# Tail of a hybrid decoder layer: a third gain product moves to GpSimd, the first gate tile's residual add is finished by ScalarE and GpSimd, and the last token tile is added in one pass of 1024 columns

## The chip, the cores and the metric

One core of one Trainium2 chip. The metric is the device time of one execution in microseconds (us), as the median over runs; lower is better.

## The reference

The layer runs an input projection into MoBA attention and gMLP gating, an output projection, a squared-ReLU MLP, and last a gated per-layer embedding (PLE). The change touches only the last of these, for 512 tokens and 1024 columns in float32:

```
gate = jax.nn.sigmoid(jnp.einsum('bsd,de->bse', h, w_ple_gate[i]) + b_ple_gate[i])
ple = jnp.einsum('bsp,pd->bsd', p[i], w_ple[i]) * gate
h = h + rms_norm(ple, ple_post_g[i])          # y * rsqrt(mean(y^2) + eps) * g
```

## The kernel before

The program is written for each engine as one fixed order of instructions, with waits on semaphores between engines. TensorE (PE) does every product in three passes (high by high, low by high, high by low part of a split float32). Nearly the whole of the kernel is a stream of such products.

The last stage works on 512 tokens as four token tiles t of 128 tokens, and on 1024 columns as two halves of W = 512. The gate product is done in seven block products of 2x2 blocks (recombined by sums and differences), each for two token tiles j; the last of them, (6, 1), is done in two parts of 256 columns. Its results come out as nine gate tiles i, numbered in the order in which they are finished:

```
GATE_TILES = ((0, 0, W), (1, 0, W), (2, W, W), (2, 0, W), (3, W, W), (0, W, W), (3, 0, W),
              (1, W, W // 2), (1, W + W // 2, W // 2))      # t, first column, width
TOKENS_DONE = (2, 0, 3, 1)                                  # order in which token tiles complete
```

So token tile 2 is gate tiles 2 and 3, token tile 0 is 0 and 5, token tile 3 is 4 and 6, and token tile 1, the last, is 1, 7 and 8. `GATE_TILES` and the names below are at L289 to L305. Each gate tile goes through these steps:

- `sigmoid(i)`, ScalarE (ACT), L2242: waits for the product in PSUM, or for `gate_c22(j)` on VectorE (tiles 2 and 4). Writes to SBUF (`acc`) for tiles 0 and 1, in place in PSUM for the others.
- `gate_ple(i)`, VectorE (DVE), L1463: times the embedding product, which was spilled to DRAM and loaded back into `ple_late` (SBUF, `ple_of(t)`).
- `square_ple(i)`, ScalarE, L1620: sum of squares (an ACTIVATE and an accumulator read). Each square waits for the one before it, since both write the same scratch tile.
- `gain_ple(i)`, VectorE, L1474: times the norm weight `ple_gain`; for tiles 0 and 1 it is `gain_by_pool(i)` on GpSimd (POOL), L2531, which writes to `ple_of(t)`.
- `partial_sum(i)` and `ple_rstd(t)`, GpSimd, L2512, L2518 and L2520: the sum of squares of a token tile to 1/sqrt of the mean. Two small instructions in `ple_rstd`, the second a power.
- `add_ple(i)`, VectorE, L1486: h = gained * rstd + h, once the token tile's `ple_rstd` is there.
- a store of the tile (L2689), issued by SyncE (SP) in the order 2, 3, 0, 5, 4, 6, 1, 7, 8, each when `out_ready` has counted that add.

What sets the order of the work is the order of these calls on each engine. VectorE also has `gate_c22(1)` (L1440), which releases gate product (5, 1) and `sigmoid(4)`, and `gate_fold(1)` (L1452, L1454), which releases product (6, 1). The calls at the end on VectorE, from `gate_ple(2)` on, are:

```
gate_ple(2) gate_fold(1) gain_ple(2) gate_c22(1) gate_ple(3) gate_ple(4) gain_ple(3) gain_ple(4)
gate_ple(5) add_ple(2) add_ple(3) gain_ple(5) gate_ple(6) add_ple(0) gate_ple(7) add_ple(5)
gain_ple(6) gate_ple(8) gain_ple(7) add_ple(4) gain_ple(8) add_ple(6) add_ple(1) add_ple(7) add_ple(8)
```

Of the kernel before, what the change touches and what calls it, by code (L numbers as in the profile page):

```python
# [35 lines left out]
ALU = mybir.AluOpType  # L36
ACT = mybir.ActivationFunctionType
AXIS_X = mybir.AxisListType.X

P = 128  # L40
# [5 lines left out]
W = 512  # L46
HALVES = D // W
# [24 lines left out]
LAST = STEPS - 1  # L72
# [16 lines left out]
GATE_COPIES = ((COPY_C11, 0), (COPY_C11, 1), (COPY_E, 0), (COPY_CHAIN, 0), (COPY_CHAIN, 1), (COPY_E, 1))  # L89
# [22 lines left out]
def gate_copy_at(which, j):  # L112

    return 3 * LAST + GATE_COPIES.index((which, j)) + 1


def gate_c22_at(j):
# [152 lines left out]
def tail_results():  # L270
# [18 lines left out]
GATE_TILES = ((0, 0, W), (1, 0, W), (2, W, W), (2, 0, W), (3, W, W), (0, W, W), (3, 0, W),  # L289
              (1, W, W // 2), (1, W + W // 2, W // 2))  # L290
TOKENS_DONE = (2, 0, 3, 1)
# [1 line left out]


LAST_GATED = len(GATE_TILES) - 1
GAINED_BY_POOL = (0, 1)


def width_of(i):
# [3 lines left out]
def gate_tiles_of(t):  # L303

    return [i for i, tile in enumerate(GATE_TILES) if tile[0] == t]  # L305
# [10 lines left out]
def hymba_layer(nc, x, xT, pT, weights, columns, rope, ws, rows, out):  # L316
# [6 lines left out]
    with ExitStack() as ctx:  # L323
# [31 lines left out]
        h = place("h", [P, TT, D])  # L355
# [65 lines left out]
        acc = place("acc", [P, TT, D], at=at_area)  # L421
# [40 lines left out]
        def ple_of(t):  # L462
            return ple_late[t // 2][:, t % 2, :]
# [16 lines left out]
        ss_pl, rstd_pl = stat[:, 146:], stat[:, 64:68]  # L480
# [11 lines left out]
        def sem(name):  # L492
            return ctx.enter_context(nc.semaphore(name))
# [9 lines left out]
        stored = sem("stored")  # L503
# [45 lines left out]
        c_summed, c_copied = sem("c_summed"), sem("c_copied")  # L549
# [4 lines left out]
        first_load = 16  # L554
        h2_raw, gate_seeded, gate_folded = sem("h2_raw"), sem("gate_seeded"), sem("gate_folded")
        h_spilled = sem("h_spilled")
        gained_by_pool = sem("gained_by_pool")
        h_loaded = [sem(f"h_loaded{t}") for t in range(TT)]
        t_hi_done, t_lo_done, a_hi_done, a_lo_done = (sem("t_hi_done"), sem("t_lo_done"),
                                                      sem("a_hi_done"), sem("a_lo_done"))  # L560
# [162 lines left out]
        def gate_result(i):  # L723

            t, c0, width = GATE_TILES[i]
            if i == LAST_GATED:
                return psum[:, GATE_LAST_PART, 0:width]
            if t < 2:
                bank = GATE_E if c0 else GATE_P1
            else:  # L730
                bank = GATE_C22 if c0 else GATE_CHAIN
            return psum[:, bank + t % 2, 0:width]

        def gated_of(i):

            t, c0, width = GATE_TILES[i]
            return acc[:, t, 0:W] if i < 2 else gate_result(i)

        def gained_of(i):

            t, c0, width = GATE_TILES[i]
            return ple_of(t)[:, c0:c0 + width] if i in GAINED_BY_POOL else gate_result(i)

        def down_result(t):

# [9 lines left out]
        def _(dve):  # L755
# [564 lines left out]
            for step in range(LAST):  # L1320
                n = PRODUCTS * step
# [135 lines left out]
            def gate_ple(i):  # L1457
                t, c0, width = GATE_TILES[i]
                cut = slice(c0, c0 + width)
                dve.wait_ge(sig_done, i + 1)  # L1460
                if i in (0, 2):
                    dve.wait_ge(ple_loaded[t // 2], 16)
                nc.vector.tensor_tensor(gated_of(i), gated_of(i), ple_of(t)[:, cut], ALU.mult).then_inc(pl_gated, 1)  # L1463

            GAINED = (2, 3, 4, 5, 6, 7, 8)

            def gain_ple(i):

                if i == GAINED[0]:
                    dve.wait_ge(post_loaded, 48)  # L1470
                t, c0, width = GATE_TILES[i]
                cut = slice(c0, c0 + width)
                dve.wait_ge(pl_squared, i + 1)
                nc.vector.tensor_tensor(gained_of(i), gated_of(i), ple_gain[:, cut], ALU.mult  # L1474
                                        ).then_inc(pl_gained, 1)

            def add_ple(i):

                t, c0, width = GATE_TILES[i]
                cut = slice(c0, c0 + width)  # L1480
                dve.wait_ge(pl_rstd, TOKENS_DONE.index(t) + 1)
                if i in GAINED_BY_POOL:
                    dve.wait_ge(gained_by_pool, GAINED_BY_POOL.index(i) + 1)
                else:
                    dve.wait_ge(pl_gained, GAINED.index(i) + 1)
                nc.vector.scalar_tensor_tensor(out=h[:, t, cut], in0=gained_of(i),  # L1486
                                               scalar=rstd_pl[:, t:t + 1], in1=h[:, t, cut],
                                               op0=ALU.mult, op1=ALU.add).then_inc(out_ready, 1)

            def tail_down(d):  # L1490

# [52 lines left out]
            h2_sum_split_lo(OF_S4, 1)  # L1544
            gate_ple(2)
            gate_fold(1)
            gain_ple(2)
            gate_c22(1)
            gate_ple(3)
            gate_ple(4)  # L1550
            gain_ple(3)
            gain_ple(4)
            gate_ple(5)
            add_ple(2)
            add_ple(3)
            gain_ple(5)
            gate_ple(6)
            add_ple(0)
            gate_ple(7)
            add_ple(5)  # L1560
            gain_ple(6)
            gate_ple(8)
            gain_ple(7)
            add_ple(4)
            gain_ple(8)
            add_ple(6)
            add_ple(1)
            add_ple(7)
            add_ple(8)

# [2 lines left out]
        def _(act):  # L1575
# [514 lines left out]
            for step in range(LAST):  # L2090
                n = PRODUCTS * step
# [143 lines left out]
            def sigmoid(i):  # L2235
                t, c0, width = GATE_TILES[i]
                j = t % 2
                if t >= 2 and c0:
                    act.wait_ge(c_summed, gate_c22_at(j))
                else:  # L2240
                    act.wait_ge(up_filled, gate_at(6 if c0 else 1 if t < 2 else 5, j) + (i == LAST_GATED))
                nc.scalar.activation(gated_of(i), gate_result(i), ACT.Sigmoid).then_inc(sig_done, 1)  # L2242

            def square_ple(i):
                t, c0, width = GATE_TILES[i]
                act.wait_ge(pl_gated, i + 1)
                square(gated_of(i), ss_pl[:, i:i + 1], pl_squared)
# [54 lines left out]
            gate_copy(COPY_E, 1)  # L2302
            square_ple(0)
            square_ple(1)
            square_ple(2)
            sigmoid(3)
            sigmoid(4)
            square_ple(3)
            square_ple(4)
            sigmoid(5)  # L2310
            square_ple(5)
            sigmoid(6)
            sigmoid(7)
            square_ple(6)
            sigmoid(8)
            square_ple(7)
            square_ple(8)


# [3 lines left out]
        def _(pool):  # L2323
# [182 lines left out]
            def partial_sum(i):  # L2506

                t = GATE_TILES[i][0]
                partial = ple_partial[:, t:t + 1]
                before = partial if i != gate_tiles_of(t)[0] else D * EPS  # L2510
                pool.wait_ge(pl_squared, i + 1)
                after(nc.gpsimd.tensor_scalar(partial, ss_pl[:, i:i + 1], before, None, ALU.add))  # L2512

            def ple_rstd(t):

                last_tile = gate_tiles_of(t)[-1]
                pool.wait_ge(pl_squared, last_tile + 1)
                after(nc.gpsimd.tensor_scalar(ple_mean, ss_pl[:, last_tile:last_tile + 1], ple_partial[:, t:t + 1],  # L2518
                                              1.0 / D, ALU.add, ALU.mult))
                nc.gpsimd.tensor_tensor(rstd_pl[:, t:t + 1], ple_mean, minus_half[:, 0:1], ALU.pow  # L2520
                                        ).then_inc(pl_rstd, 1)
                pool.wait_ge(pl_rstd, TOKENS_DONE.index(t) + 1)

            def gain_by_pool(i):
                t, c0, width = GATE_TILES[i]
                cut = slice(c0, c0 + width)
                if i == 0:
                    pool.wait_ge(post_loaded, 48)
                    pool.wait_ge(sum_lo_done, gate_sum_split_at(OF_S4, 1))
                pool.wait_ge(pl_gated, i + 1)  # L2530
                nc.gpsimd.tensor_tensor(gained_of(i), gated_of(i), ple_gain[:, cut], ALU.mult  # L2531
                                        ).then_inc(gained_by_pool, 1)

            partial_sum(0)
            partial_sum(1)
            gain_by_pool(0)
            gain_by_pool(1)
            partial_sum(2)
            ple_rstd(2)
            partial_sum(4)  # L2540
            ple_rstd(0)
            ple_rstd(3)
            partial_sum(7)
            ple_rstd(1)
# [5 lines left out]
        def _(sp):  # L2550
            for item in FIRST_ORDER:
                if isinstance(item, str):
                    i = int(item[1:])
                    t, ks = X_PIECES[i]
# [127 lines left out]
            gate_x(GATE_22, 0)  # L2682
            gate_x(GATE_22, 1)
            sp.dma_start(ple_late[1][:], ple_spill[:, 2:4, :]).then_inc(ple_loaded[1], 16)
            order = (2, 3, 0, 5, 4, 6, 1, 7, 8)
            for n, i in enumerate(order):
                t, c0, width = GATE_TILES[i]
                sp.wait_ge(out_ready, n + 1)
                sp.dma_start(out[t * P:(t + 1) * P, c0:c0 + width], h[:, t, c0:c0 + width]  # L2689
                             ).then_inc(stored, 16)  # L2690
            sp.wait_ge(stored, 16 * len(order))

# [590 lines left out]
```

## Time and profile before

| | |
|---|---|
| runs | 578.3, 579.03, 579.38 us; median 579.03 |
| profiled execution | 578.58 us, of which the span from the first to the last instruction is 576.7 us |
| PE busy | 568.4 us, 99% of the span |
| DVE busy | 500.8 us, 87% |
| ACT busy | 374.9 us, 65% |
| POOL busy | 96.2 us, 17% |
| TensorE clock | granted 0.996 of full speed over the span |

Times in the profile are us from the start of the span, durations of single instructions us or ns. In a timeline row the first number is the start, the second the duration (of the whole merged group where it says x2 and more), and what stands in brackets is the idle time of the engine before it and what ended that. VectorE and ScalarE start an instruction a little before the one in front of it has ended, so the step from start to start is shorter than a duration.

### The profile page before, as it was taken

To read this page: it belongs to the slowest core of one execution; us is meant where nothing else is said; L and a number is where in the kernel's file an instruction comes from. 1 tells how busy PE (TensorE), PEld (TensorE's weight loads), DVE (VectorE), ACT (ScalarE), POOL (GpSimd) and SP (SyncE) were. 2 spreads that over 40 slices of the span, in tenths; PEclk is the share of its full clock that TensorE was granted. 3 is DMA by queue.
4 is the path that set the end of the run, shared out by engine and by line. 5 is a ranking of instruction groups with operands and counts; after the bars stand their busy time and mean duration, and the time that the engine had idled before them with its cause. 6 is when DMAs were issued, how large, how long until landed. Compare 5 with 4: busy or idle time off the path is not lost.

```text
span 576.7 us, 8934 instructions
## 1 busy us (share of the span) xinstructions
PE 568.4 (99%) x3364; PEld 496.3 (86%) x3364; DVE 500.8 (87%) x645; ACT 374.9 (65%) x595; POOL 96.2 (17%) x159
## 2 busy tenths in 40 slices
PE   9999999999999999999999999999999999999995
PEld 7888888888888888899999989999998999988884
DVE  5899986688865998999999989999999899798898
ACT  6896674876555747667565565665665656686784
POOL 0321437000102501001000010011010100014122
PEclk9999999999999999999999999999999999999998
DMA  8982008223103497367476384592774853897823
GB/s 268 346 324 90 0 2 321 82 73 108 41 1 110 147 349 233 74 195 207 74 249 154 73 266 100 147 255 44 236 167 77 268 124 78 324 265 144 227 112 148
DMA packets 28603, 93.73 MB, mean 163 GB/s; under 512 B 3216, under 2 KB 4624, under 8 KB 28304
## 3 DMA queue, kind: packets, MB, share of 16 engines
q1 hardware_dynamic: 20736, 67.64, 33.0%
q0 software_dynamic: 5328, 19.14, 18.8%
q10 hardware_dynamic: 2496, 6.37, 3.1%
q8 instruction: 27, 0.44, 0.3%
q14 instruction: 16, 0.13, 0.1%
HBM read 86.85 MB, written 6.29 MB: 161 GB/s over the span
## 4 chain that ended last, share of the span: by engine, by line
PE 93%; DVE 3%; ACT 1%; issue 1%; DMA 1%; DVEq 0%; SPq 0%; ACTq 0%
PE psum L2703 29%; PE psum L2707 29%; PE psum L2708 29%; PE psum L2758 2%; PE psum L2941 2%; PE psum L2921 2%; DVE h L1486 1%; DMA first_raw_a<-weights_dram 1%; PE psum L2772 1%; DVE w_lo L1376 1%; DVE psum L1474 1%; DVE psum L1463 0%; ACT junk_late L1620 0%; PE psum L2795 0%; DVE actT_lo L1432 0%
## 5 line engine op out<-in xcount | busy, mean ns | idle before, releaser
L2703 PE MATMUL psum<-t_hi,a_hi 128*128 128x512 f32 x216 | 84.7, 392 | 0.0
L2707 PE MATMUL psum<-t_lo,a_hi 128*128 128x512 f32 x216 | 84.6, 392 | 0.0
L2708 PE MATMUL psum<-t_hi,a_lo 128*128 128x512 f32 x216 | 84.0, 389 | 0.0
L2703 PE MATMUL psum<-w_hi,actT_hi 128*128 128x512 f32 (+1 forms) x178 | 69.7, 392 | 0.0
L2708 PE MATMUL psum<-w_hi,actT_lo 128*128 128x512 f32 (+1 forms) x178 | 68.5, 385 | 0.0
L2707 PE MATMUL psum<-w_lo,actT_hi 128*128 128x512 f32 (+1 forms) x178 | 68.4, 384 | 0.0
L2708 PE MATMUL psum<-sum_hi,up_lo 128*128 128x256 f32 x224 | 63.4, 283 | 0.0
L2707 PE MATMUL psum<-sum_lo,up_hi 128*128 128x256 f32 x224 | 63.4, 283 | 0.0
L2703 PE MATMUL psum<-sum_hi,up_hi 128*128 128x256 f32 x224 | 63.2, 282 | 0.0
L2708 PE MATMUL psum<-actT_hi,up_lo 128*128 128x256 f32 (+1 forms) x200 | 60.0, 300 | 0.0
L2707 PE MATMUL psum<-actT_lo,up_hi 128*128 128x256 f32 (+1 forms) x200 | 60.0, 300 | 0.0
L2703 PE MATMUL psum<-actT_hi,up_hi 128*128 128x256 f32 (+1 forms) x200 | 59.9, 299 | 0.0
L2454 POOL DMA_DIRECT2D raw_x<-weights_dram x21 | 18.6, 883 | 238.6 <-DVE t_lo L1235 238.6
L1294 DVE TENSOR_TENSOR acc<-acc,psum 128x512 f32<-128x512 f32 x76 | 49.1, 681 | 1.8 <-PE psum L2708 1.8
L2708 PEld LDWEIGHTS psum<-t_hi,a_lo 128*128 128x128 f32 x216 | 40.6, 188 | 8.8
L1090 DVE TENSOR_TENSOR up_lo<-raw,up_hi 128x1024 fp32r<-128x1024 f32 x37 | 45.2, 1220 | 2.6 <-ACT up_hi L1881 2.0
L2703 PEld LDWEIGHTS psum<-t_hi,a_hi 128*128 128x128 f32 x216 | 40.8, 189 | 7.1
L2707 PEld LDWEIGHTS psum<-t_lo,a_hi 128*128 128x128 f32 x216 | 40.8, 189 | 6.6
L2707 PEld LDWEIGHTS psum<-sum_lo,up_hi 128*128 128x128 f32 x224 | 42.9, 191 | 1.1
L2703 PEld LDWEIGHTS psum<-sum_hi,up_hi 128*128 128x128 f32 x224 | 42.9, 191 | 1.1
L2708 PEld LDWEIGHTS psum<-sum_hi,up_lo 128*128 128x128 f32 x224 | 42.9, 191 | 0.0
L2707 PEld LDWEIGHTS psum<-actT_lo,up_hi 128*128 128x128 f32 x200 | 38.2, 191 | 2.0
(290 smaller groups left out, 1438.0 us busy)
## 6 DMA issues: line engine op xcount, KB each, us to landing
raw<-weights_dram SPq DMA_DIRECT2D x40, 512.0 KB, 4.8
raw_o<-weights_dram SPq DMA_DIRECT2D x23, 512.0 KB, 4.3
raw_x<-weights_dram POOLq DMA_DIRECT2D x21, 512.0 KB, 5.6
raw_second<-weights_dram SPq DMA_DIRECT2D x16, 512.0 KB, 4.1
raw_x<-weights_dram SPq DMA_DIRECT2D x9, 512.0 KB, 6.1
qk_raw<-weights_dram SPq DMA_DIRECT2D x8, 512.0 KB, 7.8
raw_o<-weights_dram POOLq DMA_DIRECT2D x7, 512.0 KB, 6.9
raw_second<-weights_dram POOLq DMA_DIRECT2D x6, 512.0 KB, 6.6
```

Source lines behind the costliest of these rows:

```text
L1090: nc.vector.tensor_tensor(up_lo[q % UP_SLOTS][:], block_source(step, j), up_hi[q % UP_SLOTS][:].bitcast(F32), ALU.subtract).then_inc(block ...
L1294: nc.vector.tensor_tensor(part, part, bank, how).then_inc(product_added, 1)
L1376: nc.vector.tensor_tensor(gate_half(low, part), gate_source(block, part), gate_half(high, part).bitcast(F32), ALU.subtract).then_inc(block ...
L1474: nc.vector.tensor_tensor(gained_of(i), gated_of(i), ple_gain[:, cut], ALU.mult).then_inc(pl_gained, 1)
L1486: nc.vector.scalar_tensor_tensor(out=h[:, t, cut], in0=gained_of(i), scalar=rstd_pl[:, t:t + 1], in1=h[:, t, cut], op0=ALU.mult, op1=ALU.a ...
L2454: nc.gpsimd.dma_start(raw_x[step % 2][:], weights[down_in_stream(step, rows, half)], accum_op=ALU.add).then_inc(x_added, 16)
L2703: begin = nc.tensor.matmul(out, a_hi, b_hi, start=first, stop=False, skip_group_check=read_between)
L2707: nc.tensor.matmul(out, a_hi, b_lo, start=False, stop=False, skip_group_check=read_between)
L2708: return nc.tensor.matmul(out, a_lo, b_hi, start=False, stop=last, skip_group_check=read_between)
L2758: mm = nc.tensor.transpose(psum[:, banks[name], j * P:(j + 1) * P], source[:, j * P:(j + 1) * P], ident[:])
L2921: mm = nc.tensor.transpose(psum[:, bank + s, k * P:(k + 1) * P], probs[:, place_in_group(unit), s, k * P:(k + 1) * P], ident[:])
L2941: mm = nc.tensor.matmul(psum[s * DH:(s + 1) * DH, BANK_O, pair * P:(pair + 1) * P], v[:, k, head * DH:(head + 1) * DH], probsT_of[place_in ...
```

## The change

`gain_ple(2)` goes from VectorE to GpSimd (`GAINED_BY_POOL` becomes (0, 1, 2)); since GpSimd reads SBUF, `gate_ple(2)` now writes to `acc`. The add of tile 0 leaves VectorE: ScalarE multiplies by rstd (`scale_gained(0)`, between `sigmoid(6)` and `sigmoid(7)`) and GpSimd adds h (`add_by_pool(0)`, between `ple_rstd(0)` and `ple_rstd(3)`). The three adds of token tile 1 become one of 1024 columns (`add_last`), for which `gain_ple(7)` and `gain_ple(8)` write to `ple_of(1)`; its store goes out as two of 512 columns, issued one behind the other. The order of the calls changes on VectorE and on ScalarE.

```diff
-GAINED_BY_POOL = (0, 1)
+GAINED_BY_POOL = (0, 1, 2)
+ADDED_BY_POOL = (0,)
+LAST_TOKENS = TOKENS_DONE[-1]
...
+            def add_last():
+                t = LAST_TOKENS
+                dve.wait_ge(pl_rstd, TOKENS_DONE.index(t) + 1)
+                dve.wait_ge(tail_by_pool, GAINED_BY_POOL.index(gate_tiles_of(t)[0]) + 1)
+                dve.wait_ge(pl_gained, len(GAINED))
+                nc.vector.scalar_tensor_tensor(out=h[:, t, :], in0=ple_of(t), scalar=rstd_pl[:, t:t + 1],
+                                               in1=h[:, t, :], op0=ALU.mult, op1=ALU.add).then_inc(out_ready, 1)
...
             gate_fold(1)
-            gain_ple(2)
+            gate_ple(3)
             gate_c22(1)
-            gate_ple(3)
+            gain_ple(3)
             gate_ple(4)
-            gain_ple(3)
-            gain_ple(4)
-            gate_ple(5)
             add_ple(2)
             add_ple(3)
+            gate_ple(5)
+            gain_ple(4)
             gain_ple(5)
             gate_ple(6)
-            add_ple(0)
+            add_ple(5)
             gate_ple(7)
-            add_ple(5)
             gain_ple(6)
+            gain_ple(7)
             gate_ple(8)
-            gain_ple(7)
             add_ple(4)
             gain_ple(8)
             add_ple(6)
-            add_ple(1)
-            add_ple(7)
-            add_ple(8)
+            add_last()
...
+            def scale_gained(i):
+                t = GATE_TILES[i][0]
+                act.wait_ge(pl_rstd, TOKENS_DONE.index(t) + 1)
...
+                nc.scalar.activation(scaled_of(i), gained_of(i), ACT.Copy, scale=rstd_pl[:, t:t + 1]
+                                     ).then_inc(c_copied, 1)
...
             square_ple(0)
             square_ple(1)
+            sigmoid(3)
             square_ple(2)
-            sigmoid(3)
+            square_ple(3)
             sigmoid(4)
-            square_ple(3)
             square_ple(4)
             sigmoid(5)
             square_ple(5)
             sigmoid(6)
+            scale_gained(0)
             sigmoid(7)
             square_ple(6)
+            square_ple(7)
             sigmoid(8)
-            square_ple(7)
             square_ple(8)
...
+            def add_by_pool(i):
+                t, c0, width = GATE_TILES[i]
+                cut = slice(c0, c0 + width)
+                pool.wait_ge(c_copied, GATE_SCALED + ADDED_BY_POOL.index(i))
+                nc.gpsimd.tensor_tensor(h[:, t, cut], scaled_of(i), h[:, t, cut], ALU.add
+                                        ).then_inc(tail_by_pool, 1)
...
             partial_sum(2)
+            gain_by_pool(2)
             ple_rstd(2)
             partial_sum(4)
             ple_rstd(0)
+            add_by_pool(0)
             ple_rstd(3)
...
-            order = (2, 3, 0, 5, 4, 6, 1, 7, 8)
+            order = (2, 3, 5, 0, 4, 6)
...
+            sp.wait_ge(out_ready, len(added_by_dve) + 1)
+            for half in range(HALVES):
+                cut = slice(half * W, (half + 1) * W)
+                sp.dma_start(out[LAST_TOKENS * P:(LAST_TOKENS + 1) * P, cut], h[:, LAST_TOKENS, cut]
+                             ).then_inc(stored, 16)
```

## Rows read from the trace of the kernel before

**Rows 1.** The page: busy time of two engines over the span.

```profile
PE 568.4 (99%) x3364; PEld 496.3 (86%) x3364; DVE 500.8 (87%) x645; ACT 374.9 (65%) x595; POOL 96.2 (17%) x159
```

**Rows 2.** Timeline of TensorE: last matmuls of products (4,1) and (6,1).

```profile
561.04 0.39 PE L2708 MATMUL psum<-w_hi,actT_lo 128*128 128x512 f32 x1
...
569.46 0.28 PE L2708 MATMUL psum<-w_hi,actT_lo 128*128 128x256 f32 x1
```

**Rows 3.** Timeline of VectorE from 560 us to its end.

```profile
560.26 0.42 DVE L1454 TENSOR_TENSOR psum<-psum,acc 128x256 f32<-128x256 f32 x1
...
561.54 0.70 DVE L1440 TENSOR_TENSOR psum<-acc,psum 128x512 f32<-128x512 f32 x1
562.14 1.44 DVE L1463 TENSOR_TENSOR psum<-psum,ple_late_b 128x512 f32<-128x512 f32 x2
563.59 1.48 DVE L1474 TENSOR_TENSOR psum<-psum,ple_gain 128x512 f32<-128x512 f32 x2
564.98 0.69 DVE L1463 TENSOR_TENSOR psum<-psum,ple_late_a 128x512 f32<-128x512 f32 x1
565.57 1.40 DVE L1486 SCALAR_TENSOR_TENSOR h<-psum,stat,h 128x512 f32<-128x512 f32 x2
...
571.70 0.42 DVE L1474 TENSOR_TENSOR psum<-psum,ple_gain 128x256 f32<-128x256 f32 x1
572.03 0.74 DVE L1486 SCALAR_TENSOR_TENSOR h<-psum,stat,h 128x512 f32<-128x512 f32 x1
572.69 0.74 DVE L1486 SCALAR_TENSOR_TENSOR h<-ple_late_a,stat,h 128x512 f32<-128x512 f32 x1
573.35 0.87 DVE L1486 SCALAR_TENSOR_TENSOR h<-psum,stat,h 128x256 f32<-128x256 f32 x2
```

**Rows 4.** Timeline of ScalarE over the same stretch (L2242 sigmoid, L1620 square).

```profile
565.70 0.60 ACT L1620 ACTIVATE junk_late<-psum 128x512 f32<-128x512 f32 x1 [0.88 <-DVE psum L1463]
566.19 0.19 ACT L1620 ACTIVATION_READ_ACCUMULATOR junk_late<-psum 128x1 f32 x1
566.91 0.58 ACT L2242 ACTIVATE psum<-psum 128x512 f32<-128x512 f32 x1 [0.52 <-PE psum L2708]
568.34 0.37 ACT L2242 ACTIVATE psum<-psum 128x256 f32<-128x256 f32 x1 [0.85 <-PE psum L2708]
```

**Rows 5.** Timeline of GpSimd (L2531 gain_by_pool, L2512 partial_sum, L2518 and L2520 ple_rstd).

```profile
559.64 2.55 POOL L2531 TENSOR_TENSOR ple_late_a<-acc,ple_gain 128x512 f32<-128x512 f32 x2 [0.17 <-POOL stat L2512]
562.16 0.21 POOL L2512 TENSOR_SCALAR stat<-stat 128x1 f32<-128x1 f32 x1
563.73 0.27 POOL L2518 TENSOR_SCALAR stat<-stat 128x1 f32<-128x1 f32 x1 [1.35 <-ACT junk_late L1620]
564.08 0.57 POOL L2520 TENSOR_TENSOR stat<-stat 128x1 f32<-128x1 f32 x1
571.83 0.57 POOL L2520 TENSOR_TENSOR stat<-stat 128x1 f32<-128x1 f32 x1
```

**Rows 6.** Groups by line and shape: two forms that the change adds.

```profile
L1395 DVE SCALAR_TENSOR_TENSOR acc<-acc,stat,mlp_gain 128x1024 f32<-128x1024 f32 x1 | 1.3, 1284 | 0.7 <-POOL stat L2354 0.7
L1586 ACT ACTIVATE w_hi<-raw,cols x32: 706/713/730, 18.1 to 141.9; 128x512 fp32r<-128x512 f32 x32
```

**Rows 7.** Timeline of the SP queue: the first store's issue, and the last two.

```profile
566.34 0.34 SPq L2689 DMA_DIRECT2D out_dram<-h  x1
573.86 0.94 SPq L2689 DMA_DIRECT2D out_dram<-h  x2
```

**Rows 8.** DMA issues in the last 4 us: size of each, us to landing.

```profile
out_dram<-h SPq DMA_DIRECT2D x2, 256.0 KB, 2.0
out_dram<-h SPq DMA_DIRECT2D x2, 128.0 KB, 2.1
```

**Rows 9.** Stretches: busy us of PE, PEld, DVE, ACT, POOL; clock; DMA share, GB/s.

```profile
566.30:567.10 0.80, 0.80 (x7) 0.72 (x6) 0.80 (x3) 0.28 (x2) 0.46 (x2) 1.00 0.00 0
567.10:567.80 0.70, 0.70 (x9) 0.70 (x8) 0.70 (x2) 0.39 (x1) 0.38 (x1) 1.00 0.88 345
```

More of the change, by code:

```diff
@@ L114, in gate_copy_at @@
     return 3 * LAST + GATE_COPIES.index((which, j)) + 1
+GATE_SCALED = 3 * LAST + len(GATE_COPIES) + 1
 def gate_c22_at(j):
@@ L295 @@
 LAST_GATED = len(GATE_TILES) - 1
-GAINED_BY_POOL = (0, 1)
+GAINED_BY_POOL = (0, 1, 2)
+ADDED_BY_POOL = (0,)
+LAST_TOKENS = TOKENS_DONE[-1]
+GAINED = (3, 4, 5, 6, 7, 8)
 def width_of(i):
@@ L556, in hymba_layer @@
         h_spilled = sem("h_spilled")
-        gained_by_pool = sem("gained_by_pool")
+        tail_by_pool = sem("tail_by_pool")
         h_loaded = [sem(f"h_loaded{t}") for t in range(TT)]
@@ L736, in gated_of, with sigmoid_of, scaled_of @@
             t, c0, width = GATE_TILES[i]
+            if i == 2:
+                return acc[:, t, c0:c0 + width]
             return acc[:, t, 0:W] if i < 2 else gate_result(i)
+        def sigmoid_of(i):
+            return gated_of(i) if i < 2 else gate_result(i)
         def gained_of(i):
             t, c0, width = GATE_TILES[i]
-            return ple_of(t)[:, c0:c0 + width] if i in GAINED_BY_POOL else gate_result(i)
+            kept = i in GAINED_BY_POOL or t == LAST_TOKENS
+            return ple_of(t)[:, c0:c0 + width] if kept else gate_result(i)
+        def scaled_of(i):
+            t, c0, width = GATE_TILES[i]
+            return ple_of(t)[:, c0:c0 + width]
         def down_result(t):
@@ L1462, in gate_ple @@
                     dve.wait_ge(ple_loaded[t // 2], 16)
-                nc.vector.tensor_tensor(gated_of(i), gated_of(i), ple_of(t)[:, cut], ALU.mult).then_inc(pl_gated, 1)
-            GAINED = (2, 3, 4, 5, 6, 7, 8)
+                nc.vector.tensor_tensor(gated_of(i), sigmoid_of(i), ple_of(t)[:, cut], ALU.mult).then_inc(pl_gated, 1)
             def gain_ple(i):
@@ L1482, in add_ple @@
                 if i in GAINED_BY_POOL:
-                    dve.wait_ge(gained_by_pool, GAINED_BY_POOL.index(i) + 1)
+                    dve.wait_ge(tail_by_pool, GAINED_BY_POOL.index(i) + 1)
                 else:
@@ L2241, in sigmoid @@
                     act.wait_ge(up_filled, gate_at(6 if c0 else 1 if t < 2 else 5, j) + (i == LAST_GATED))
-                nc.scalar.activation(gated_of(i), gate_result(i), ACT.Sigmoid).then_inc(sig_done, 1)
+                nc.scalar.activation(sigmoid_of(i), gate_result(i), ACT.Sigmoid).then_inc(sig_done, 1)
+            def scale_gained(i):
+                t = GATE_TILES[i][0]
+                act.wait_ge(pl_rstd, TOKENS_DONE.index(t) + 1)
+                if i in GAINED_BY_POOL:
+                    act.wait_ge(tail_by_pool, GAINED_BY_POOL.index(i) + 1)
+                else:
+                    act.wait_ge(pl_gained, GAINED.index(i) + 1)
+                nc.scalar.activation(scaled_of(i), gained_of(i), ACT.Copy, scale=rstd_pl[:, t:t + 1]
+                                     ).then_inc(c_copied, 1)
             def square_ple(i):
@@ L2531, in gain_by_pool @@
                 nc.gpsimd.tensor_tensor(gained_of(i), gated_of(i), ple_gain[:, cut], ALU.mult
-                                        ).then_inc(gained_by_pool, 1)
+                                        ).then_inc(tail_by_pool, 1)
+            def add_by_pool(i):
+                t, c0, width = GATE_TILES[i]
+                cut = slice(c0, c0 + width)
+                pool.wait_ge(c_copied, GATE_SCALED + ADDED_BY_POOL.index(i))
+                nc.gpsimd.tensor_tensor(h[:, t, cut], scaled_of(i), h[:, t, cut], ALU.add
+                                        ).then_inc(tail_by_pool, 1)
             partial_sum(0)
@@ L2684, in _ @@
             sp.dma_start(ple_late[1][:], ple_spill[:, 2:4, :]).then_inc(ple_loaded[1], 16)
-            order = (2, 3, 0, 5, 4, 6, 1, 7, 8)
-            for n, i in enumerate(order):
+            order = (2, 3, 5, 0, 4, 6)
+            added_by_dve = [i for i in order if i not in ADDED_BY_POOL]
+            for i in order:
                 t, c0, width = GATE_TILES[i]
-                sp.wait_ge(out_ready, n + 1)
+                if i in ADDED_BY_POOL:
+                    sp.wait_ge(tail_by_pool, len(GAINED_BY_POOL) + ADDED_BY_POOL.index(i) + 1)
+                else:
+                    sp.wait_ge(out_ready, added_by_dve.index(i) + 1)
                 sp.dma_start(out[t * P:(t + 1) * P, c0:c0 + width], h[:, t, c0:c0 + width]
                              ).then_inc(stored, 16)
-            sp.wait_ge(stored, 16 * len(order))
+            sp.wait_ge(out_ready, len(added_by_dve) + 1)
[3 more added lines that the diff above has]
+                             ).then_inc(stored, 16)
+            sp.wait_ge(stored, 16 * (len(order) + HALVES))
         @block.tensor
```

## The prediction

> **What bounds the kernel now.** I read the page first: TensorE is busy for 99% of the span [rows 1]. So only the time behind its last product can change, unless the edit makes TensorE wait. Next the timeline of TensorE: the last matmul starts at 569.46 and ends at 569.74 [rows 2], and the span ends at 576.7. What lies in those 7 us is the drain of the last tiles. The timeline of VectorE [rows 3] shows it working almost without a gap from 560 us to its last add, which ends at 573.35 + 0.87 = 574.22. GpSimd's last `ple_rstd` ends at 571.83 + 0.57 = 572.40 [rows 5], while the first add that needs it starts only at 572.69 [rows 3]: VectorE's backlog, by 0.3 us, and not the norm, sets the end. The SP queue issues the last store at about 574.34 (the last two issues take 0.94 together from 573.86, some 0.45 of it the second) [rows 7]; it lands 2.0 to 2.1 later, at 576.4 [rows 8], and the span ends 0.3 after that.
>
> **Prices from the rows.** VectorE, from start to start: 0.60 for 512 columns of tensor_tensor (561.54 to 562.14), 0.33 for 256 (571.70 to 572.03), 0.66 for an add of 512 (572.69 to 573.35) [rows 3]. ScalarE [rows 4]: sigmoid 0.58, of 256 columns 0.37; a square of 512 is complete 0.68 after its start (565.70 to 566.38), and the next instruction that isn't a square starts some 0.1 before that. GpSimd: a product of 512 columns 1.26 from start to start (559.64 to 562.16 for two), `ple_rstd` 0.92 from its first start to the end of its power (563.73 to 564.65) [rows 5]. A wait between engines costs 0.04, and 0.17 into GpSimd (566.38 is the square's end in [rows 4]; the 0.17 is the bracket of the first row in [rows 5]).
>
> **What is removed.** From VectorE: `gain_ple(2)` 0.60, `add_ple(0)` 0.66, and the three last adds, 0.66 + 0.87 = 1.53, become one of 1024 columns. The trace has that form at L1395, 1.28 [rows 6], so 0.25 less. In all 1.51 us of VectorE's work. If that were all, the last add would end at 572.7.
>
> **Why it can't end there.** The last rstd is not made by VectorE. Its chain is last matmul 569.74, sigmoid(8), gate_ple(8), square_ple(8), `ple_rstd(1)`, and it ended at 572.40 [rows 5], 2.66 after the matmul, with nothing in it that the edit shortens. `add_last` needs it before its first column. So it ends at 572.40 + 0.05 + 1.28 = 573.73 at best, 0.5 before today's 574.22, and not 1.5.
>
> **What the new order does, step by step.** I place each instruction behind its engine's last one and behind its releaser.
>
> VectorE to 564.7: `gate_fold(1)` as before, its second part at 560.26 [rows 3]; `gate_ple(3)` 560.59 (sigmoid(3) now runs before square_ple(2), so it is there); `gate_c22(1)` at 561.54 as before, because product (4, 1) ends at 561.04 + 0.39 = 561.43 [rows 2]; so the place freed by `gain_ple(2)` is partly empty already. `gain_ple(3)` 562.14, `gate_ple(4)` at 562.88, as before (the second of the pair from 562.14 ends at 563.58 and takes 0.70, it waits for sigmoid(4)) [rows 3]. Now comes `add_ple(2)`, which waits for `ple_rstd(2)`. On GpSimd the new product fills the gap in front of it: `partial_sum(2)` 562.16, `gain_by_pool(2)` 562.45 to 563.7, `ple_rstd(2)` 563.71 to 564.64, the time it also had before (564.08 + 0.57) [rows 5]. So GpSimd pays nothing for the gain, but VectorE, which had two gains and `gate_ple(5)` in front of this add, has nothing: it stands idle from 563.48 to 564.70, 1.2 us. Queued behind are add 2, add 3 and, behind these, `gate_ple(5)`, at 564.70 + 2 x 0.66 = 566.02 in place of 564.98 [rows 3].
>
> For `gate_ple(5)` wait square_ple(5) and all that stands behind it on ScalarE. Square 566.74 to 567.43 (before 565.70 to 566.38) [rows 4]. `ple_rstd(0)` 567.60 to 568.52. sigmoid(6) 567.33 to 567.91. `scale_gained(0)` waits for that rstd: 568.56. Its form, Copy with a scale per partition, stands at L1586 with 0.71 [rows 6]: to 569.27. Queued behind it is sigmoid(7), at 569.18 against 568.34 before [rows 4], then square_ple(6) 569.46 to 570.15, square_ple(7) 570.23 to 570.69, sigmoid(8) 570.58 to 570.95. The last product is there at 569.74, so sigmoid(8) is 0.8 late.
>
> VectorE meanwhile: `gain_ple(4)` 566.62, `gain_ple(5)` 567.47 (waits for its square, 0.25 idle), `gate_ple(6)` 568.07, add 5 568.67, `gate_ple(7)` 569.59 (waits for sigmoid(7)), `gain_ple(6)` 570.19 (square_ple(6)), `gain_ple(7)` 570.79, `gate_ple(8)` 571.12 to 571.55. Square_ple(8) is complete at 572.04.
>
> GpSimd: `add_by_pool(0)` after scale_gained, 569.44 to 570.70. The trace has no GpSimd add, but a product of the same shape with the same two SBUF inputs [rows 5]; I take 1.26, with 0.9 and 1.6 as the ends; VectorE gets to add 4 at 571.45, so that the shorter gains only 0.2 and the longer costs 0.34. Behind it is `ple_rstd(3)`, 570.70 to 571.62; add 4 waits for it, at 571.66. Then `gain_ple(8)` 572.32, add 6 572.65, `add_last` at 573.31. `ple_rstd(1)` (572.21 to 573.13) is in time for it. It ends at 573.31 + 1.28 = **574.59, 0.37 later than before**: 1.5 us of work removed; 1.2 us of idle ahead of add 2 and 1.0 in four small waits (ahead of `gain_ple(5)`, `gate_ple(7)`, `gain_ple(6)` and add 4) put in; the rest, some 0.3, are small waits that the old order had. TensorE isn't touched: `gate_c22(1)` and `gate_fold(1)`, which release its last products, stay where they were.
>
> **The stores.** The first half is issued at 574.62, the second 0.34 to 0.45 behind it (the length of an issue) [rows 7]. A store of 256 KB alone lands after 2.0 [rows 8]: nothing moves for 0.8 us after the issue at 566.34, then the engines fill [rows 9]. The 345 GB/s of the next stretch at a share of 0.88 [rows 9] make some 390 at full share, by which 256 KB need 0.67 us, so the second half waits for the first and lands some 2.0 + 0.65 = 2.65 after the first issue; without that queueing at 2.34. So 576.96 to 577.3, I take 577.25. Before, the last piece was 128 KB, landing at 576.4, 2.2 behind its add. Cost of the stores: 0.04 + 2.65 against 2.2: 0.5.
>
> The Trainium skill (DMA: Bandwidth & Descriptors, Anatomy of one DMA) fits a DMA as a fixed 2.0 us plus bytes over 436 GB/s; a 256 KB store would land after 2.6 by it, and both halves after some 3.2. The trace has 2.0 and 2.1 for 256 and 128 KB, where the rule would want 0.3 between them, so I go by the rows.
>
> **Sum.** Against the profiled execution: +0.37 for the last add, +0.5 for the stores, some +0.85 in all: a span of 577.5, and 579.4 for its execution, which lay 0.45 under the median. Against the median 579.03 it is 579.03 + 0.8 = **579.8 us**. What a measurement of this kernel can tell from no change is 0.2%, or 1.16 us, so this is "no change", on its slow side.
>
> **Rivals.** (1) *VectorE packs without the waits.* From add 2 at 564.70 the remaining work is 5 adds (3.3), 5 products of 512 (3.0), 4 of 256 (1.3) and the 1.28: 8.9, so 573.6; with the floor 573.73 and stores of 2.65 it gives 576.4, the same as before: -0.3 to +0.3, 579.0. For it: each small wait is 0.2 to 0.3 and could vanish. Against: scale_gained(0) can't run before the chain through `gate_ple(5)`, which is late for certain. Chance 0.16.
> (2) *Slower by more than 0.2%: GpSimd becomes the bound.* It now carries 2.5 us more at two places on which an idle VectorE waits: each 0.1 us that `gain_by_pool(2)` takes above 1.26 delays `ple_rstd(2)` and add 2 by as much, and all behind them. It decides from 0.31 us on: 0.85 + 0.31 = 1.16. If both took 1.6 it would be 0.34 at each, 579.03 + 0.85 + 0.68 = 580.6. Against: the two products of before took 1.26 each beside a busy VectorE [rows 5]. Chance 0.15. The Trainium skill (GPSIMD Engine Reference, Specifications) says that GpSimd shares its SBUF interfaces with VectorE and contends with VectorE instructions that have two SBUF inputs; VectorE has none such beside either of the new ones in the order above.
> (3) *The two halves add their whole latency.* If the second lands 3.3 after the first issue, the end is 0.65 later, +1.5 us, 580.5. The landing of 2.0 for a lone 256 KB speaks against it [rows 8]; the skill's rule above would come near it. Chance 0.06.
> (4) *Faster by over 0.2%.* It takes the last add and the last landing to be 1.16 earlier, below the floor of 573.73 + 2.38, 576.1, which is only 0.3 under today's 576.4. Only a spread between runs could show it. Chance 0.04.
> The forecast itself, +0.3 to +1.15, has 0.59.
>
> **The numbers.** Faster 0.04. Same: 0.59 + 0.16 and 0.01 of the rest, 0.76. Slower: 0.20. The range takes in rival 1 below and most of 2 and 3 above, and the 578.3 to 579.38 of the runs: 578.5 to 580.7.
>
> **What would show it.** Right: VectorE idle by about 1.2 us ahead of the first L1486 row, released by GpSimd; sigmoid(7) some 0.8 later than 568.34, behind an ACTIVATE of 0.7; the 1024-column add of about 1.28 starting at or after 573.0; a second store landing about 2.65 after the first issue; TensorE's last matmul unmoved. Wrong: TensorE's end moves (a late `gate_fold` or `gate_c22`), the idle ahead of add 2 is under 0.5, or the 1024-column add starts by 572.6.

## The result and the profile after

| | us |
|---|---|
| before, 20 runs | median 578.59 (578.18 to 580.02) |
| changed, 20 runs | median 579.57 (578.99 to 580.5) |
| ratio | 1.0016, 95% interval 1.001 to 1.0022 |
| profiled execution of the changed kernel | 580.29, span 578.5 |

The changed kernel is slower by 0.16%, some 0.9 us. That is clear of zero, and inside the 0.2% up to which the prediction counted "no change".

The timeline of VectorE after (L1483 is `gate_ple`, L1492 `gain_ple`, L1504 `add_ple`, L1514 `add_last`, L1460 `gate_c22`); it answers to [rows 3]:

```profile
560.27 0.68 DVE L1483 TENSOR_TENSOR acc<-psum,ple_late_b 128x512 f32<-128x512 f32 x1
...
562.13 0.68 DVE L1460 TENSOR_TENSOR psum<-acc,psum 128x512 f32<-128x512 f32 x1
563.04 0.70 DVE L1492 TENSOR_TENSOR psum<-psum,ple_gain 128x512 f32<-128x512 f32 x1 [0.23 <-ACT junk_late L1643]
563.65 0.69 DVE L1483 TENSOR_TENSOR psum<-psum,ple_late_b 128x512 f32<-128x512 f32 x1
565.63 0.75 DVE L1504 SCALAR_TENSOR_TENSOR h<-ple_late_b,stat,h 128x512 f32<-128x512 f32 x1 [1.30 <-POOL stat L2554]
566.30 0.74 DVE L1504 SCALAR_TENSOR_TENSOR h<-psum,stat,h 128x512 f32<-128x512 f32 x1
566.97 0.69 DVE L1483 TENSOR_TENSOR psum<-psum,ple_late_a 128x512 f32<-128x512 f32 x1
...
570.53 0.43 DVE L1483 TENSOR_TENSOR psum<-psum,ple_late_a 128x256 f32<-128x256 f32 x1 [0.17 <-ACT psum L2265]
...
572.54 0.75 DVE L1504 SCALAR_TENSOR_TENSOR h<-psum,stat,h 128x512 f32<-128x512 f32 x1
...
574.20 1.28 DVE L1514 SCALAR_TENSOR_TENSOR h<-ple_late_a,stat,h 128x1024 f32<-128x1024 f32 x1
```

The row to see first is the add at 565.63. In its bracket stand 1.30 us of idle time, ended by GpSimd: add 2 waits for `ple_rstd(2)`. The `gate_ple(5)` at 566.97 stands behind it in VectorE's queue. The timelines of ScalarE and GpSimd show where that goes (L2265 sigmoid, L2274 `scale_gained`, L2565 `gain_by_pool`, L2572 `add_by_pool`, L2554 the power of `ple_rstd`); they answer to [rows 4, 5]:

```profile
567.69 0.60 ACT L1643 ACTIVATE junk_late<-psum 128x512 f32<-128x512 f32 x1 [2.14 <-DVE psum L1483]
...
568.27 0.59 ACT L2265 ACTIVATE psum<-psum 128x512 f32<-128x512 f32 x1
569.50 0.72 ACT L2274 ACTIVATE ple_late_a<-ple_late_a,stat 128x512 f32<-128x512 f32 x1 [0.64 <-POOL stat L2554]
570.13 0.36 ACT L2265 ACTIVATE psum<-psum 128x256 f32<-128x256 f32 x1
```

```profile
563.40 1.30 POOL L2565 TENSOR_TENSOR ple_late_b<-acc,ple_gain 128x512 f32<-128x512 f32 x1
564.67 0.27 POOL L2552 TENSOR_SCALAR stat<-stat 128x1 f32<-128x1 f32 x1
565.03 0.57 POOL L2554 TENSOR_TENSOR stat<-stat 128x1 f32<-128x1 f32 x1
...
570.37 1.26 POOL L2572 TENSOR_TENSOR h<-ple_late_a,h 128x512 f32<-128x512 f32 x1 [0.90 <-ACT ple_late_a L2274]
```

ScalarE sits idle for 2.14 us until `gate_ple(5)` comes, then for 0.64 until the norm of token tile 0 is there, and only behind `scale_gained(0)` comes sigmoid(7). GpSimd has no idle time between its product and `ple_rstd(2)`: the product stands right in front of it.

At the end the timeline of the SP queue (L2741 issues the two halves of the last store), and that line's durations in ns, starts and times to landing, answering to [rows 7, 8]:

```profile
575.51 0.81 SPq L2741 DMA_DIRECT2D out_dram<-h  x2
```

```profile
L2741 SPq DMA_DIRECT2D out_dram<-h x2: 333/383/433, 575.5 to 575.9; - x2
...
DMA to landing us min/median/max: 2.0/2.1/2.2
```

The add ends at 574.20 + 1.28 = 575.48, the halves are issued at 575.5 and 575.9, and the second takes 2.2 to land.

To set this profile against the one of before, two marks are wanted. The timeline of TensorE has its last matmul, answering to [rows 2]:

```profile
569.93 0.28 PE L2760 MATMUL psum<-w_hi,actT_lo 128*128 128x256 f32 x1
```

It ends at 570.21, 0.47 later than before, and `gate_ple(2)` starts at 560.27, 0.94 later (559.33 in the trace of before). Neither is the change's doing. Long before its place, an accumulating load of gate weights (issued by GpSimd at 527.1, 512 KB) landed later in this execution, and ScalarE and VectorE, and in the end TensorE's weight load, waited for it. The DMA issues (KB, us to landing), the timeline of ScalarE and VectorE, and the waits (us in total, times, longest):

```profile
raw_second<-weights_dram POOLq DMA_DIRECT2D x1, 512.0 KB, 12.9
```

```profile
540.09 1.06 ACT L2169 ACTIVATE w_hi<-raw_second 128x1024 fp32r<-128x1024 f32 x1 [1.50 <-DMA raw_second<-weights_dram]
...
541.18 1.22 DVE L1396 TENSOR_TENSOR w_lo<-raw_second,w_hi 128x1024 fp32r<-128x1024 f32 x1 [1.87 <-ACT w_hi L2169]
```

```profile
PEld psum L2755 <- DVE actT_lo L1452: 0.8, 1, 0.8
```

In the profile of before the same load landed after 11.7 us and ScalarE waited for 0.28. The timelines of ScalarE and VectorE there (L1463 is `gate_ple`):

```profile
539.14 1.06 ACT L2146 ACTIVATE w_hi<-raw_second 128x1024 fp32r<-128x1024 f32 x1 [0.28 <-DMA raw_second<-weights_dram]
...
540.23 1.22 DVE L1376 TENSOR_TENSOR w_lo<-raw_second,w_hi 128x1024 fp32r<-128x1024 f32 x1 [0.65 <-ACT w_hi L2146]
...
559.33 0.69 DVE L1463 TENSOR_TENSOR psum<-psum,ple_late_b 128x512 f32<-128x512 f32 x1
```

VectorE's row at 541.18 stands at 540.23 here, so the whole delay, 0.95, is present before the first instruction that the change touches. Four kernels below (two adds, both mends, rstd first, product doubled), which have the same order of work up to here, but whose load landed after 10.9 to 12.1, start their last matmul at 569.32 to 569.44 against 569.46 before, and the profile shows no wait of TensorE for another engine from 545 us on. The reordered kernel and that with tile 0 on VectorE, where it landed after 12.6 and 12.4, start it late, like the changed one, at 570.20 and 570.05. The profiled execution, 580.29, lies 0.7 above its own median; the late load is the likely reason, but the other executions left no profile that could show it. In the text below, times in the tail are given against the end of the last matmul, or against `gate_ple(2)`, and each says which.

### The profile page after: what moved, and what is told of

Same layout as the page of the kernel before. It is cut to its first block, busy times and chain, and to the rows that moved or that the text cites. A ratio compares the mean times of both kernels' runs of the same rounds, so it can differ in the third digit from the quotient of the medians.

```text
span 578.5 us, 8930 instructions
## 1 busy us (share of the span) xinstructions
PE 568.6 (98%) x3364; PEld 496.4 (86%) x3364; DVE 499.5 (86%) x641; ACT 375.4 (65%) x596; POOL 99.3 (17%) x161
## 4 chain that ended last, share of the span: by engine, by line
PE 86%; DMA 3%; DVE 3%; ACT 2%; POOL 2%; issue 1%; DVEq 0%; POOLq 0%; ACTq 0%
PE psum L2755 27%; PE psum L2759 26%; PE psum L2760 26%; DMA raw_second<-weights_dram 2%; PE psum L2993 2%; PE psum L2810 2%; PE psum L2973 2%; DMA raw<-weights_dram 1%; DVE w_lo L1396 1%; PE psum L2864 1%; ACT w_hi L2169 1%; PE psum L2824 1%; POOL ple_late_a L2565 0%; POOL stat L2388 0%; PE psum L2847 0%
```

## The experiments

Eight kernels were timed, each against runs of the kernel before on the same chip, in 11 or 12 runs each, the doubled product in 5. Theory 1 is the prediction's own: an idle VectorE ahead of add 2, with `gate_ple(5)` and the chain to sigmoid(7) behind it, costs upstream, and the stores cost at the end. "Behind" is the end of the last add less the end of the last matmul, and "tail" the end of the span less that of the last matmul.

| kernel | ratio to before, interval | behind | tail |
|---|---|---|---|
| before | | 4.48 | 6.96 |
| changed | 1.0016, 1.001 to 1.0022 | 5.27 | 8.29 |
| reordered | 0.9997, 0.9988 to 1.0006 | 4.05 | 7.12 |
| tile 0 on VectorE | 1.002, 1.001 to 1.0029 | 5.31 | 8.37 |
| last add alone | 1.0006, 0.9997 to 1.0015 | 4.23 | 7.24 |
| two adds | 1.0008, 0.9999 to 1.0017 | 5.30 | 7.70 |
| reordered, two adds | 0.9984, 0.9975 to 0.9993 | 3.99 | 6.40 |
| rstd first, two adds | 0.9988, 0.9979 to 0.9997 | 4.09 | 6.48 |
| product doubled | 1.0033, 1.0021 to 1.0046 | 6.09 | 9.15 |
| product alone | 1.0000, 0.9991 to 1.0009 | 4.48 | 7.05 |

**Reordered.** The changed kernel with two VectorE instructions moved:

```diff
             gate_ple(4)
+            gain_ple(4)
+            gate_ple(5)
             add_ple(2)
             add_ple(3)
-            gate_ple(5)
-            gain_ple(4)
             gain_ple(5)
```

> The changed kernel with gain_ple(4) and gate_ple(5) ahead of add_ple(2) on VectorE, as in the order of before. Theory 1 (the loss upstream is VectorE idling ahead of add_ple(2) for ple_rstd(2), with gate_ple(5) and the whole chain to sigmoid(7) queued behind it): most of that idle is filled, scale_gained(0) and sigmoid(7) come some 1 us earlier against the last matmul, the 1024-column add starts on the release of the last ple_rstd, 4.0 us or less after the end of the last matmul less its own 1.28, i.e. it ends 3.9 to 4.2 us behind the last matmul instead of 5.3; the time is 0.9 us under the changed kernel, about that of before (ratio to before 0.999 to 1.001). Rival (the detour of tile 0 over ScalarE and GpSimd costs the time by itself): idle goes, but the last add still ends over 4.8 behind the last matmul, ratio 1.001 to 1.002.

VectorE's timeline:

```profile
565.38 0.70 DVE L1492 TENSOR_TENSOR psum<-psum,ple_gain 128x512 f32<-128x512 f32 x1 [0.75 <-ACT junk_late L1643]
565.99 0.69 DVE L1483 TENSOR_TENSOR psum<-psum,ple_late_a 128x512 f32<-128x512 f32 x1
566.59 0.74 DVE L1504 SCALAR_TENSOR_TENSOR h<-ple_late_b,stat,h 128x512 f32<-128x512 f32 x1
...
573.25 1.28 DVE L1514 SCALAR_TENSOR_TENSOR h<-ple_late_a,stat,h 128x1024 f32<-128x1024 f32 x1
```

Add 2 no longer waits; 0.75 are left ahead of `gain_ple(4)`, which needs its square. The last add ends 4.05 behind the last matmul, in the middle of the forecast, with the detour of tile 0 untouched. It starts right behind add 6 and not on the release of the last norm, as expected, which had ended 0.14 earlier. The median is 578.37 against 578.49 of before: the order of two instructions was all of the loss upstream. The rival's 1.001 to 1.002 lie above the interval, and it falls.

**Tile 0 on VectorE.** The changed kernel without the detour:

```diff
-ADDED_BY_POOL = (0,)
+ADDED_BY_POOL = ()
...
             gate_ple(6)
+            add_ple(0)
+            gate_ple(7)
             add_ple(5)
-            gate_ple(7)
...
             sigmoid(6)
-            scale_gained(0)
             sigmoid(7)
...
             ple_rstd(0)
-            add_by_pool(0)
             ple_rstd(3)
...
-            order = (2, 3, 5, 0, 4, 6)
+            order = (2, 3, 0, 5, 4, 6)
```

> The changed kernel with tile 0's add back on VectorE (scale_gained and add_by_pool gone, add_ple(0) behind gate_ple(6)). Theory 1: the detour only occupies engines that wait anyway, since gate_ple(5) is late in both; sigmoid(7) comes earlier but VectorE has 0.66 more to do, so the last add ends within 0.2 us of where it ends in the changed kernel, 5.1 to 5.4 behind the last matmul, ratio to before 1.001 to 1.002. Rival (the detour is what costs): last add at least 0.5 earlier, ratio 1.000 to 1.001.

VectorE's timeline, `gate_ple(7)` and the last add:

```profile
570.39 0.43 DVE L1483 TENSOR_TENSOR psum<-psum,ple_late_a 128x256 f32<-128x256 f32 x1
...
574.36 1.28 DVE L1514 SCALAR_TENSOR_TENSOR h<-ple_late_a,stat,h 128x1024 f32<-128x1024 f32 x1
```

The last add ends 5.31 behind, against 5.27, and the ratio is 1.002. So the detour neither costs nor saves here. The 0.66 it takes from VectorE comes back as waits: in the changed kernel VectorE stands for 0.26 ahead of `gate_ple(7)`, 0.27 ahead of `gain_ple(6)` and 0.14 ahead of add 4, and here ahead of none of the three.

**Last add alone.** The kernel before with only `add_last` and its two stores (and `gain_ple(7)`, `gain_ple(8)` writing to `ple_of(1)`):

```diff
             add_ple(6)
-            add_ple(1)
-            add_ple(7)
-            add_ple(8)
+            add_last()
...
-            order = (2, 3, 0, 5, 4, 6, 1, 7, 8)
+            order = (2, 3, 0, 5, 4, 6)
...
+            for half in range(HALVES):
+                cut = slice(half * W, (half + 1) * W)
+                sp.dma_start(out[P:2 * P, cut], h[:, 1, cut]).then_inc(stored, 16)
...
```

> The kernel before with only the last part of the change: one add of 1024 columns for token tile 1 and two stores of 512 columns behind it. Theory 1: the add starts where the first of the three did (behind add_ple(6), about 2.95 us after the end of the last matmul) and ends 0.25 us earlier than the three did, but both halves are stored behind it, the second lands some 2.65 behind the first issue against 2.2 behind the last add before; net +0.2 to +0.3 us, ratio 1.0000 to 1.0008. Rival (the single pass and wide stores pay): -0.25 us, ratio 0.9992 to 1.000.

VectorE's timeline:

```profile
573.01 1.28 DVE L1496 SCALAR_TENSOR_TENSOR h<-ple_late_a,stat,h 128x1024 f32<-128x1024 f32 x1
```

The single pass ends 4.23 behind in place of 4.48, 0.25 earlier as priced; the tail is 0.28 longer all the same. The ratio's interval holds 1, so the sign rests on the two profiles, where the size is the one forecast.

**Two adds.** The changed kernel with the last tile in two passes:

```diff
-                nc.vector.scalar_tensor_tensor(out=h[:, t, :], in0=ple_of(t), scalar=rstd_pl[:, t:t + 1],
-                                               in1=h[:, t, :], op0=ALU.mult, op1=ALU.add).then_inc(out_ready, 1)
+                for half in range(HALVES):
+                    cut = slice(half * W, (half + 1) * W)
+                    nc.vector.scalar_tensor_tensor(out=h[:, t, cut], in0=ple_of(t)[:, cut], scalar=rstd_pl[:, t:t + 1],
+                                                   in1=h[:, t, cut], op0=ALU.mult, op1=ALU.add).then_inc(out_ready, 1)
...
-            sp.wait_ge(out_ready, len(added_by_dve) + 1)
             for half in range(HALVES):
+                sp.wait_ge(out_ready, len(added_by_dve) + half + 1)
```

> The changed kernel with the last tile added in two passes of 512 columns, each stored behind its own. Theory 1 (the stores cost because both wait for the whole add): the first half is issued 0.6 us earlier, the second add ends 0.12 later than the single pass, the second store is not queued behind the first and lands 2.0 after its issue: the end comes 0.5 us earlier against the last matmul than in the changed kernel; ratio to before about 1.0005 to 1.001. Rival (the stores' landing is fixed and the number of issues counts): no change or +0.1 us, ratio 1.0016.

The last add ends where it did (5.30; counted from `gate_ple(2)`, 15.33 against 15.21, it is the 0.12 later that was expected), but the tail is 7.70 and not 8.29: 0.59 less. The ratio, 1.0008, is in the range of theory 1, but its interval reaches 1.0017 and so holds the rival's 1.0016: what decides is the two profiles. The timeline of the SP queue, and the same line's durations, starts and landings:

```profile
574.26 0.99 SPq L2743 DMA_DIRECT2D out_dram<-h  x2
```

```profile
L2743 SPq DMA_DIRECT2D out_dram<-h x2: 332/332/332, 574.3 to 574.9; - x2
...
DMA to landing us min/median/max: 2.0/2.0/2.0
```

Issued 0.66 apart, each half lands after 2.0; issued 0.4 apart, the second took 2.2. The second half is issued 5.3 behind the last matmul in place of 5.7: of what is won, 0.4 is the earlier issue and 0.2 the shorter landing.

**Both mends together.** The edits of "reordered" and of "two adds" in one kernel.

> Both mends together: the changed kernel with gain_ple(4) and gate_ple(5) ahead of add_ple(2), and the last tile added in two passes of 512 columns with a store behind each. Theory 1 (the two costs are separate and add up): last add some 4.2 us behind the last matmul, its store lands 2.0 after its issue, the span ends 6.4 to 6.6 behind the last matmul against 6.96 before; ratio to before 0.999 to 0.9995. Rival (the tail is bound by something neither edit touches): no better than the reordered kernel alone, ratio 0.9995 to 1.0003.

Rows of the timelines of ScalarE, GpSimd (the last norm), VectorE and SP:

```profile
568.30 0.37 ACT L2267 ACTIVATE psum<-psum 128x256 f32<-128x256 f32 x1
...
571.68 0.57 POOL L2556 TENSOR_TENSOR stat<-stat 128x1 f32<-128x1 f32 x1
...
572.28 1.41 DVE L1516 SCALAR_TENSOR_TENSOR h<-ple_late_a,stat,h 128x512 f32<-128x512 f32 x2
...
573.06 0.99 SPq L2743 DMA_DIRECT2D out_dram<-h  x2
```

Sigmoid(7) is back at 568.30 (568.34 before), the first of the last adds starts at 572.28. The tail is 6.40 where 6.4 to 6.6 was forecast, 0.56 shorter than before. The runs, 577.71 to 578.06, lie all below the lowest of the kernel before beside them, 578.22. The ratio, 0.9984, is 0.0006 better than the best expected; the profiles account for 0.56 us of the 0.8 between the medians, and where the rest comes from stays open.

**Rstd first.** `gain_by_pool(2)` behind `ple_rstd(2)`, and VectorE's order to suit, with the two adds:

```diff
-            gain_by_pool(2)
             ple_rstd(2)
+            gain_by_pool(2)
...
             gate_ple(4)
-            add_ple(2)
             add_ple(3)
-            gate_ple(5)
             gain_ple(4)
+            gate_ple(5)
+            add_ple(2)
             gain_ple(5)
...
-            order = (2, 3, 5, 0, 4, 6)
+            order = (3, 2, 5, 0, 4, 6)
```

> The changed kernel with ple_rstd(2) ahead of gain_by_pool(2) on GpSimd, add 3 in the gap on VectorE, then gain_ple(4), gate_ple(5), add 2; and the last tile in two passes. Theory 1: ple_rstd(2) ends 1.3 us earlier (it waited on GpSimd only for the product in front of it), add 3 fills the gap, gate_ple(5) is back at its old place; from there the floor of the last ple_rstd sets the end, so it equals the run with both mends within 0.2 us, ratio 0.999 to 0.9995. Rival (ple_rstd(2) is bound by its square and not by the product): ple_rstd(2) no earlier, add 3 waits 1 us, ratio 1.000 to 1.001.

The timelines of GpSimd and, for the last adds, of VectorE:

```profile
562.85 0.27 POOL L2554 TENSOR_SCALAR stat<-stat 128x1 f32<-128x1 f32 x1
563.20 0.57 POOL L2556 TENSOR_TENSOR stat<-stat 128x1 f32<-128x1 f32 x1
563.85 1.30 POOL L2567 TENSOR_TENSOR ple_late_b<-acc,ple_gain 128x512 f32<-128x512 f32 x1
...
571.70 0.57 POOL L2556 TENSOR_TENSOR stat<-stat 128x1 f32<-128x1 f32 x1
```

```profile
571.74 0.74 DVE L1504 SCALAR_TENSOR_TENSOR h<-psum,stat,h 128x512 f32<-128x512 f32 x1
572.40 1.41 DVE L1516 SCALAR_TENSOR_TENSOR h<-ple_late_a,stat,h 128x512 f32<-128x512 f32 x2
```

On GpSimd the norm now ends at 563.77, 4.07 behind `gate_ple(2)` (559.70) where it was 5.33 (565.60 less 560.27): 1.26 earlier, just the product. It was the product, not the square, that held it. The time is about that of the kernel with both mends (0.9988 against 0.9984, again a little better than the range expected, but with an interval that reaches into it). The last norm ends 2.55 behind the last matmul in both. There the first of the last adds starts 0.03 behind it, on the floor; here it starts 0.13 behind it, at 572.40, right behind add 6. So with both mends in, an earlier `ple_rstd(2)` finds nothing left to win.

**Product doubled.** The changed kernel with `gain_by_pool(2)` issued twice, to the same place, the second behind the end of the first:

```diff
+                if i == 2:
+                    after(nc.gpsimd.tensor_tensor(gained_of(i), gated_of(i), ple_gain[:, cut], ALU.mult))
```

> The changed kernel with gain_by_pool(2) issued twice. Theory 1 (add_ple(2) waits on GpSimd's queue, without slack, and all behind it with it): VectorE's idle ahead of add_ple(2) grows from 1.3 to 2.6 us, the last add ends 1.2 to 1.4 later against the last matmul, ratio to before 1.0035 to 1.0042. Rival (the idle is slack that later work takes up): last add under 0.5 later, ratio 1.0016 to 1.0025.

VectorE's timeline:

```profile
561.45 0.70 DVE L1460 TENSOR_TENSOR psum<-acc,psum 128x512 f32<-128x512 f32 x1 [0.33 <-PE psum L2762]
...
565.90 0.75 DVE L1504 SCALAR_TENSOR_TENSOR h<-ple_late_b,stat,h 128x512 f32<-128x512 f32 x1 [2.41 <-POOL stat L2554]
...
574.47 1.27 DVE L1514 SCALAR_TENSOR_TENSOR h<-ple_late_a,stat,h 128x1024 f32<-128x1024 f32 x1
```

The idle time ahead of add 2 is 2.41, where 2.6 was expected. Counted from `gate_ple(2)` (559.17 here) the last add ends after 16.57, against 15.21: 1.36 later, in full. Counted from the last matmul it is only 0.82 later, less than the 1.2 expected, because VectorE as a whole ran earlier in this execution: the accumulating load had landed after 10.9. The time is some 1.0 above the changed kernel's by the ratios (1.0033 less 1.0016), between the theories and nearer to the first. Counted from `gate_ple(2)`, a delay on GpSimd passes through to the last add without slack; the time agrees, but its interval (1.0021 to 1.0046) holds part of the rival's range too.

**Product alone.** The kernel before with only `gain_ple(2)` moved to GpSimd, ahead of `ple_rstd(2)`:

```diff
-GAINED_BY_POOL = (0, 1)
+GAINED_BY_POOL = (0, 1, 2)
...
             gate_fold(1)
-            gain_ple(2)
             gate_c22(1)
```

> The kernel before with only gain_ple(2) moved to GpSimd, ahead of ple_rstd(2), all else in the old order. Theory 1: the 0.60 us taken from VectorE buys nothing, since gate_c22(1) behind it waits for product (4, 1), and gain_ple(3), gain_ple(4) wait for ScalarE; add 2 starts no more than 0.1 earlier, ratio 0.9995 to 1.0003. Rival (VectorE's work counts in full up to the floor of the last ple_rstd): last add 0.3 us earlier, ratio 0.999 to 0.9997.

VectorE's timeline:

```profile
561.35 0.70 DVE L1446 TENSOR_TENSOR psum<-acc,psum 128x512 f32<-128x512 f32 x1 [0.93 <-PE psum L2714]
...
565.39 0.74 DVE L1492 SCALAR_TENSOR_TENSOR h<-ple_late_b,stat,h 128x512 f32<-128x512 f32 x1
```

Where the product stood, VectorE now waits 0.93 for TensorE. Add 2 starts 4.16 ahead of the end of the last matmul, 4.17 before. The last add ends 4.48 behind, as before, and the ratio is 1.0000. Its interval, down to 0.9991, doesn't exclude the rival's 0.3 us by itself; the place of the last add does. Relief of 0.60 on VectorE bought nothing.

## Why the prediction was right

579.8 was forecast, 579.57 measured; the step from before to after was put at +0.8 to +0.85, and it is +0.9 by the ratio. That the totals are as close as 0.2 has some luck in it: the forecast stood on a median of before of 579.03, from 3 runs, and over 20 runs it is 578.59. Had it stood on that, it would have been 579.4, as near from below. The mechanism does not hang on it. Point by point:

- *The bound and the floor.* TensorE was not delayed by the edit. Its end did move by 0.47 in the profiled execution, which the prediction listed as a sign of being wrong; but it waited for the late load, and not for a late `gate_fold` or `gate_c22`, and in the four kernels named above it did not move. The floor under `add_last` held: the best two kernels start their last add 0.03 behind `ple_rstd(1)` or right behind add 6, none earlier. Its size was 0.11 too large, 2.55 from the last matmul to the last norm and not 2.66: before, `gate_ple(8)` stood a little in VectorE's queue. In the changed kernel that norm ends 3.87 behind, far above the floor.
- *The idle ahead of add 2.* 1.2 forecast, 1.30 in the bracket, released by GpSimd. Undoing it alone gave 1.2 back (5.27 to 4.05), doubling its cause added 1.36.
- *The chain.* From `gate_ple(2)`, which starts 0.94 later than the prediction's 559.33, the steps fell where they were placed: add 2 at 564.69 (564.70 forecast), `gate_ple(5)` 566.03 (566.02), `scale_gained(0)` 568.56 (568.56), sigmoid(7) 569.19 (569.18), add 4 571.60 (571.66), the last add's end 574.54 (574.59).
- *Prices.* The GpSimd add, which no row of before had, took 1.26 as assumed, and the product beside it in the change 1.30; the scaled copy 0.72 against 0.71; the pass of 1024 columns 1.28. So neither of GpSimd's new instructions ran longer than forecast by more than 0.04.
- *The stores.* The last landing was forecast 2.65 behind the first issue; the halves were issued some 0.4 apart and the second landed after 2.2, so 2.6. From the last add to the end of the span it is 3.02 against 2.48 before: 0.54 for the stores, 0.5 forecast. The prediction also weighed a fit of the Trainium skill (DMA: Bandwidth & Descriptors, Anatomy of one DMA), by which it would have been 3.2. The page gives that fit for DMAs issued by GpSimd, which the prediction did not say, and these stores are issued by SyncE: their 2.6 shows that it can't be carried over to them, and tests nothing of it where it was made.
- *The rivals.* VectorE packing without waits did not happen in the changed kernel, but is nearly what "reordered" does, with the ratio that rival 1 gave. GpSimd as the bound was a matter of degree: it is on the chain, at its usual speed.

What was off: the wait ahead of add 4 was put at 0.2, and it was 0.14 (the four small waits together 0.92, 1.0 forecast); and the profile's own span, 578.5, is 1.0 over the 577.5 forecast, of which the late load, which no step of the prediction considered, made 0.94. Counted from `gate_ple(2)` that drops out: the last add ends 15.21 behind it in place of 14.89, so 0.32 later where 0.37 was forecast.

## What to carry to other kernels

Work taken from a busy engine is worth what the next wait allows: place each instruction behind its engine's last one and behind its releaser, and look at which wait takes up the gap before counting the microseconds removed. A first-in first-out queue makes an instruction that waits for a slow side chain hold everything behind it, so what feeds other engines goes ahead of what only finishes a tile. At the very end, split the last work by what can be stored early: two passes cost 0.13 us more than one here, and ended 0.59 us sooner.

## What the runs showed of the hardware

The landing of one 512 KB accumulating load, issued by GpSimd beside other loads, varied between 10.3 and 12.9 us over the ten profiles of kernels that are the same up to there (11.7 in before, 12.9 in the changed one, 10.9 with the product doubled, 10.3 with the product alone). VectorE's whole tail moved with it. In two kernels with the same order of work up to there, VectorE waited 0.33 for TensorE ahead of `gate_c22(1)` where the load took 10.9, and where it took 12.9 it did not, and a TensorE weight load had waited 0.8 for VectorE. A single profile of this kernel can't be compared by its span to better than about 1 us.
